# A hybrid decoder step: cache copies, low rank part and first loads moved in the RWKV stage

## The reference

```python
prev = concatenate([shift0[:, None, :], pa[:, :-1]], axis=1)
m = pa + (prev - pa) * mu
r, k, v, xw, xa, xg = split_last(m, A_SPLIT)
wlog = -softplus(-(w0 + tanh(xw) @ w2)) - 0.5
decay = exp(-exp(wlog))
a = sigmoid(a0 + xa @ a2)
g = sigmoid(xg) @ g2
...
S = S * w_t - s_kk * (kk_t * a_t) + v_t * k_t
y_t = S @ r_t
```

## Time and profile before

| what | us |
| --- | --- |
| three runs: median (lowest, highest) | 3149.25 (3148.3, 3158.02) |
| the profiled execution: its time, its span | 3146.62, 3144.8 |
| TensorE busy in the span | 2659.9 |
| VectorE, ScalarE, GpSimd busy | 1142.1, 666.5, 370.1 |

### The profile page before, as it was taken

One profiled execution on the slowest core, in us unless ns is written; L12 is line 12 of the kernel. 1 busy time (PEld: TensorE's weight loads), 2 busy tenths in 40 slices (PEclk: granted clock), 3 DMA queues, 4 the chain that ended last, 5 costly groups with the idle time before them and its releaser, 6 DMA issues. The chain is left out here.

```text
span 3144.8 us, 33977 instructions
## 1 busy us (share of the span) xinstructions
PE 2659.9 (85%) x13604; PEld 1693.4 (54%) x13604; DVE 1142.1 (36%) x2070; ACT 666.5 (21%) x1339; POOL 370.1 (12%) x352
## 2 busy tenths in 40 slices
PE   7999995084788888686647759999999999999998
PEld 3444441042567778354425425566666666888843
DVE  0007999565676664485704203200000000000033
ACT  1122221032334444474403200000000000000011
POOL 1000000102443441000016520000000000000000
PEclk9999997586799999798868879999999999999999
DMA  6111110322235343513779772311101102110010
GB/s 237 51 44 49 42 41 17 116 83 53 58 112 172 101 146 111 164 40 90 244 246 346 274 289 100 132 29 40 40 27 40 40 27 93 51 37 22 17 34 33
DMA packets 170291, 305.86 MB, mean 97 GB/s; under 512 B 48536, under 2 KB 121448, under 8 KB 167866
## 3 DMA queue, kind: packets, MB, share of 16 engines
q1 hardware_dynamic: 145154, 175.87, 17.9%
q0 software_dynamic: 23136, 93.01, 8.1%
q10 hardware_dynamic: 1864, 35.08, 3.2%
HBM read 262.76 MB, written 68.29 MB: 105 GB/s over the span
## 5 line engine op out<-in xcount | busy, mean ns | idle before, releaser
L929 PE MATMUL m_B<-m_big,m_wdB 128*128 128x363 f32 (+1 forms) x2112 | 646.0, 468 | 3.2 <-issue 3.2
L929 PEld LDWEIGHTS m_B<-m_big,m_wdB 128*128 128x128 f32 x2112 | 400.4, 190 | 247.9 <-issue 4.8
L384 PE MATMUL i_psM<-i_w,i_xnT 128*128 128x477 f32 x1024 | 418.3, 567 | 2.3 <-ACT i_xnT L232 2.3
L384 PEld LDWEIGHTS i_psM<-i_w,i_xnT 128*128 128x128 f32 x1024 | 192.8, 191 | 213.4 <-issue 206.5
L791 DVE TENSOR_TENSOR m_actT<-m_wdB,m_B 128x363 f32 (+3 forms) x66 | 35.1, 532 | 604.1 <-PE m_B L929 604.1
L683 ACT ACTIVATE m_wdB<-m_B 128x363 f32<-128x363 f32 (+1 forms) x66 | 31.2, 473 | 598.8 <-PE m_B L929 598.8
L971 PE MATMUL m_B<-m_wdA,m_actT 128*128 128x256 f32 x704 | 152.4, 379 | 0.8 <-DVE m_actT L791 0.8
L971 PE MATMUL m_B<-m_wdB,m_actT 128*128 128x256 f32 x704 | 152.6, 379 | 0.0
L971 PEld LDWEIGHTS m_B<-m_wdA,m_actT 128*128 128x128 f32 x704 | 133.7, 190 | 19.5 <-DVE m_actT L791 1.4
L971 PEld LDWEIGHTS m_B<-m_wdB,m_actT 128*128 128x128 f32 x704 | 133.5, 190 | 18.8 <-issue 0.8
L649 POOL TENSOR_TENSOR m_rstd<-m_ms,m_half 128x1 f32<-128x1 f32 x18 | 10.0, 553 | 1133.0 <-DVE m_ms L759 1133.0
(11 more groups left out here) (410 smaller groups left out, 3599.9 us busy)
## 6 DMA issues: line engine op xcount, KB each, us to landing
b_Kp<-b_k SPq DMA_DIRECT2D x32, 512.0 KB, 10.9
b_Vp<-b_v SPq DMA_DIRECT2D x32, 512.0 KB, 11.4
o_bk<-b_k ACTq DMA_DIRECT2D x8, 2040.0 KB
o_bv<-b_v ACTq DMA_DIRECT2D x8, 2040.0 KB
i_w<-w_in POOLq DMA_DIRECT2D x8, 1908.0 KB, 29.9
proj<-i_stage SPq DMA_DIRECT2D x64, 238.5 KB, 2.0
m_wdB<-w_gate SPq DMA_DIRECT2D x22, 512.0 KB, 4.0
m_wdB<-w_up SPq DMA_DIRECT2D x22, 512.0 KB, 5.2
```

The source lines that it names most:

```text
L384: mm = nc.tensor.matmul(psM[:, c % 2, 0:CHW], xnT[:, t % 2, k, :], w[:, k, c * CHW:(c + 1) * CHW], start=(k == 0), stop=(k == KO - 1))
L929: mm = nc.tensor.matmul(B[:, bank, 0:r1 - r0], wgu[:, i, u, k, :], hnT[:, k, r0:r1], start=(k == 0), stop=(k == KO - 1))
```

## The change

Six edits, all in the mix phase:

1. `load_first` moves ahead of the table's store in the indexer, and the loads of the eight old states follow it there.
2. The first difference (VectorE) and its multiply by mu (GpSimd) move from the start of `phase_rwkv` into the indexer.
3. In ScalarE's tile the copy of W stands between B and q, and for j of 1 and up the low rank activations follow behind q.
4. The cache copies are issued behind the sigmoid of w, ahead of the levels, in place of the end of the tile.
5. `warm`, an exponential of one column, follows the gate's copy at level 2, so that the exponential table is loaded there.
6. TensorE's pieces 0, 1 and 2 of the next tile's low rank part each move one place later, and VectorE's copies `turned` move behind the masks.

```diff
+        self.st_in = sb("st_in", [P, 4, H_A, 64])
...
+    def load_states(self, sp):
+        for n in range(N_SEQ):
+            sp.dma_start(self.st_in[64 * (n % 2):64 * (n % 2) + 64, n // 2, :, :],
+                         self.D["wkv"][n].rearrange("h v k -> v h k")).then_inc(self.S["st_in"], 16)
+
+    def first_difference(self, dve):
+        dve.wait_ge(self.S["cur_in"], 16)
+        dve.wait_ge(self.S["prev_in"], 16 * (N_SEQ + 1))
+        self.nc.vector.tensor_tensor(self.prev[0:64, :], self.prev[0:64, :], self.cur[0:64, :], ALU.subtract)\
+            .then_inc(self.S["d"], 1)
+
+    def first_shift(self, pool):
+        pool.wait_ge(self.S["mu_in"], 16)
+        pool.wait_ge(self.S["d"], 1)
+        self.nc.gpsimd.tensor_tensor(self.prev[0:64, :], self.prev[0:64, :], self.mu[0:64, :], ALU.mult)\
+            .then_inc(self.S["dmu"], 1)
...
                 load(1)
-                for n in range(N_SEQ):
-                    sp.dma_start(st_in[64 * (n % 2):64 * (n % 2) + 64, n // 2, :, :],
-                                 D["wkv"][n].rearrange("h v k -> v h k")).then_inc(S["st_in"], 16)
...
-                pool.wait_ge(S["mu_in"], 16)
-                shift(0)
+                count["dmu"] = 1
...
+                def warm():
+                    f(tiny[:, :], half[:, 0:1], ACT.Exp)
...
-                    if nxt:
-                        lora_of(j + 1)
-                    evac_bq(j)
+                    if j == 0:
+                        lora_of(1)
+                    evac_bq(j, 0)
                     if j >= 1:
                         evac_w(first(old))
+                    evac_bq(j, 1)
+                    if j >= 1:
+                        if nxt:
+                            lora_of(j + 1)
                         evac_u(first(old), old, 0)
                         evac_y(first(old), old, 0)
...
                     if nxt:
                         sig_w(j + 1)
+                    if j >= 1:
+                        move_caches(j - 1)
                     for lev in range(last + 1):
...
                         if lev == 2 and nxt:
                             gate(j + 1)
+                            warm()
...
-                    if j >= 1:
-                        move_caches(j - 1)
...
-                differ(0)
                 select(1)
                 mix(0)
...
                     evac_pr(j)
+                    if j == 0:
+                        turned(1)
                     if nxt:
-                        turned(j + 1)
                         keys(j + 1)
                     mask(j)
+                    if j and nxt:
+                        turned(j + 1)
...
                     elif where == "turned2":
                         if j >= 1:
                             solve(old, 0)
-                        if nxt:
-                            front(j + 1, 0)
+                        elif nxt:
+                            front(1, 0)
                     elif where == "matted":
                         if j == 0:
...
+                            front(1, 1)
                         else:
+                            if nxt:
+                                front(j + 1, 0)
                             close(old, 0)
-                        if nxt:
-                            front(j + 1, 1)
                     elif where == (0, 0):
...
                         if nxt:
-                            front(j + 1, 2)
+                            front(j + 1, 1 if j else 2)
                     elif where == (0, 1):
                         if j >= 2:
                             old_part(old, 1)
+                        if nxt and j:
+                            front(j + 1, 2)
...
                 sp.dma_start(cmask[:, :], D["cmask"]).then_inc(cmask_in, 16)
+                mix_.load_first(sp)
+                mix_.load_states(sp)
                 sp.wait_ge(summed, TCH)
                 sp.dma_start(D["table"], table[:, :]).then_inc(table_out, 16)
-                mix_.load_first(sp)
...
+                mix_.first_shift(pool)
...
+                mix_.first_difference(dve)
                 for q in range(NQ):
```

More of the change, by code:

```diff
@@ L1079, in __init__ @@
         self.score = self.room[0:64, :]
-        names = "cur_in prev_in mu_in vec_in small_in lw_in last_in round unsel unsel_out score_out table_out".split()
+        self.st_in = sb("st_in", [P, 4, H_A, 64])
+        names = "st_in d dmu cur_in prev_in mu_in vec_in small_in lw_in last_in round unsel unsel_out score_out table_out".split()
         self.S = {n: nc.alloc_semaphore("a_" + n) for n in names}
         self.nc, self.D = nc, D
+    def load_states(self, sp):
[12 more added lines that the diff above has]
+            .then_inc(self.S["dmu"], 1)
     def load_first(self, sp):
@@ L1146, in phase_rwkv @@
         masks = [at("mask_s"), at("mask")]
-        half = sb("half", [P, H_A])
+        half, tiny = sb("half", [P, H_A]), sb("tiny", [P, 1])
         lora = sb("lora", [P, P])
@@ L1169, in phase_rwkv @@
         mean, var, rstd = (sb(n, [P, H_A]) for n in ("mean", "var", "rstd"))
-        st_in = sb("st_in", [P, 4, H_A, 64])
+        st_in = mix_.st_in
         STs = sb("STs", [P, 4, N_SEQ, 64])
@@ L1178, in phase_rwkv @@
         S = {n: sem(n) for n in (
-            "st_in n_in v_in d dmu m lora loraT lT z sig cum exps kk sq ssk "
+            "n_in v_in m lora loraT lT z sig cum exps kk sq ssk "
             "rsk kkn k2 p r b q rk bonus pown own owned bq pr evacB evacP mat mats LT1 L xt0 low vb lnb Wdone W Udone U Sdone "
@@ L1440, in exp_end, with evac_bq @@
                         .then_inc(S["exps"], 1)
-                def evac_bq(j):
+                def evac_bq(j, x):
                     n = chunks(j)
[L1444 to L1448, removed]
+                    act.wait_ge(S["bq"], 2 * j + x + 1)
+                    src = B[:, 2 + x, 0:256 * n].rearrange("p (i c t) -> p i c t", i=4, c=n)
+                    f(BQ[0:64, :, 0:n, x, :], src[0:64], ACT.Copy).then_inc(S["evacB"], 1)
+                    f(BQ[64:P, :, 0:n, 1 - x, :], src[64:P], ACT.Copy).then_inc(S["evacB"], 1)
+                def warm():
+                    f(tiny[:, :], half[:, 0:1], ACT.Exp)
                 def evac_w(k):
```

## The result

| | before | changed |
|---|---|---|
| first runs, median (lowest to highest), us | 3152.96 (3148.3 to 3158.02), 4 runs | 3128.36 (3124.85 to 3129.63), 4 runs |
| profiled execution's own time, us | 3146.62 | 3129.59 |
| its span, us | 3144.8 | 3127.8 |
| RWKV stage in it, us | 543.0 | 521.4 |

The account below looks back on a forecast made before the run. No engine fills the RWKV stage, so its order decides. Terms −3.5 − 10.8 − 3.5 + 0.4 − 1.9 give −19 on 3146.6, 3128, plus 1.3 toward the median: 3129 us; own range 3120 to 3139, stated range 3114 to 3144.

Parts of the forecast that it names:

- Indexer, nothing: Indexer: early loads, states, difference and multiply fit where engines already wait or idle; cost nothing.
- Start, −3.5: RWKV stage's start: VectorE's first difference (1.92) and wait (1.58) go, so m of the sample rows comes 3.5 us earlier.
- taken as worth nothing: Stage start: moving the state loads alone gains nothing, since one DMA engine carries the shifted rows; bounds 0 and 3.4 us.
- Tile 1, 0; tile 2, +0.4; tile 3, −3.5: Whole tiles: tile 1's 1.1 and 1.4 cancel; tile 2 loses 0.4 us; tile 3 gains 3.5, its start giving 3.8.
- Tiles 4 to 7, −2.7 each, −10.8: Each tile: start gains 3.0 us, exponential table 1.4; VectorE's low rank copies cost 0.6, moved low rank products 1.1.
- The cache copies, hidden by 1 us: ScalarE between sigmoid of w and first X copy: that copy ends at 3.2, TensorE wants it at 4.2.
- Tail, −1.9: Behind the last tile: TensorE's 2.01 us wait while ScalarE issues copies ahead of W goes, but for W's copy waiting its turn.
- the states were the wait: Rival, stage start: state packets hold up the shifted rows; moving them frees TensorE's 23.79 us too, 3105; chance 0.06.
- The tile start gains nothing: Rival, tile starts: half-speed products or VectorE eat the 3.0 us; 3146 against the median; chance 0.17.
- The clock stays up: Rival, tile starts: shorter idle leaves the clock at 1.00, masks another us earlier in tiles 3 to 7; 3122; chance 0.15.
- The half clock reaches into the levels: Rival, slower: half speed eats the 3.0 us and costs 3.4 in the levels of tiles 3 to 8; 3166; chance 0.07.
- The table load: Rival, ScalarE behind the gate: the load holds it as long again, exceeding the gap by 0.7 in seven tiles; 3134; chance 0.04.

Follow-up runs that it names:

- states_back: Changed kernel with the eight old-state loads put back behind the loads of tile 1, all else kept; 3127.74 us, ratio 0.9926.
- no_warm: Changed kernel without the one-column exponential behind the gate's copy; 3136.8 us, ratio 0.9955.
- lowrank_back: Changed kernel with the low rank part back in its old place on ScalarE, TensorE and VectorE; 3121.69 us, ratio 0.9903.
- copies_end: Changed kernel with the four cache copies issued at the end of a tile again; 3130.26 us, ratio 0.9938.
- start_only: Kernel before with only the start part: early first loads and states, first difference and its multiply in the indexer; 3150.72 us, ratio 0.9996.
- three: Changed kernel plus tile 1's shifted rows loaded in two parts, VectorE's last two finishing operations behind level 0, low rank part in its old place; 3082.29 us.
- split_load: Changed kernel with the shifted rows of tile 1 loaded as 112 and 15 rows instead of 127 in one; 3105.63 us, ratio 0.9858.

## Why the prediction was right, point by point

The number, the direction and what bounds the stage, TensorE's waits, were right; the steps less evenly so.

- *Indexer, nothing.* Right: the stage in front of RWKV ends 0.4 us later in the profiled execution (728.8 for 728.4), no more than the difference between executions: the kernels with the same indexer end it between 728.1 and 730.2.
- *Start, −3.5.* Measured −4.9: 3.4 from the difference and the wait, and 1.5 from the states, within their bounds of 0 to 3.4 (states_back: 1.6).
- *Tile 0.* Here the sum had no term, and this is the step that failed: the state move was "taken as worth nothing", by bounds that only allowed a gain. It cost: tile 0 got 3.3 us longer at half clock, and with the states put back the stage is 3.0 shorter, in the profiles; the times of the two kernels are the same (3128.36 and 3127.74 us). The turned states, which had stood behind TensorE's long wait, now stand ahead of it.
- *Tile 1, 0; tile 2, +0.4; tile 3, −3.5.* Measured 0, +0.9, −5.1. In tile 3 the start gave 4.0 us for the 3.8 forecast; the excess is clock, the B products took 3.68 us before and 2.06 now.
- *Tiles 4 to 7, −2.7 each, −10.8.* Measured −3.2, −2.9, −2.6 and −1.4, together −10.1. In tile 4 the terms show singly: start −2.9 for −3.0; exponential table −1.3 for −1.4 (no_warm: 8.4 us over the stage); the moved product +1.1, confirmed by lowrank_back. VectorE's low rank copies cost the 0.6 forecast: from the end of the masks to the first X it needs 1014.56 − 1012.71 = 1.85 us before and 1006.33 − 1003.85 = 2.48 now. The first X still comes 2.7 us earlier in the tile, because the B products took 0.43 us less, a term that the sum did not have. Over tiles 4 to 7 that term is −0.4, +0.2, +0.5 and +0.5, and tile 7's start gave only 2.0. VectorE, before and then in the changed kernel:

```profile
1014.56 0.68 DVE L1677 TENSOR_TENSOR a_X<-a_B,a_smalls 128x512 f32<-128x512 f32 x1
```

```profile
1002.56 1.29 DVE L1691 TENSOR_TENSOR a_mats<-a_B,a_smalls 128x512 f32<-128x512 f32 x2 [0.38 <-PE a_B L1845]
...
1006.33 0.67 DVE L1699 TENSOR_TENSOR a_X<-a_B,a_smalls 128x512 f32<-128x512 f32 x1
```

- *The cache copies, hidden by 1 us.* Right: they end at 1013.65 in tile 4 and no wait of TensorE is put down to X there; copies_end shows the same from the other side.
- *Tail, −1.9.* The wait of 2.01 us is gone, but tile 8 and the tail give 5.7 in all. Nearly all the rest is clock: the B products of tile 8 took 3.79 us before and 3.28 now, the sixteen products of its level 0 3.65 and 2.27, the products behind the tail's U 2.00 and 1.25, and the old-state products after them 1.80 and 1.15. The level 0 products, before and now:

```profile
1218.88 3.65 PE L1821 MATMUL a_B<-a_X,a_LT 128*128 128x128 f32 x16 [0.59 <-DVE a_X L1677]
```

```profile
1202.32 2.27 PE L1845 MATMUL a_B<-a_X,a_LT 128*128 128x128 f32 x16 [0.58 <-DVE a_X L1699]
```

So the overshoot at the start, in tile 3 and in the tail and the missing loss in tile 0 nearly cancel: −21.6 for −19 in the stage. The forecast also stood on 3147.9 us for the kernel before, 2 to 5 us under its later medians, which hides the rest. That the time came out within 1 us of 3129 is luck to that extent. That the change gains some 20 us is not: 15.2 of the 21.6 lie in tiles 3 to 7, for which 14.3 were forecast.

Of the rivals, "the states were the wait" fell in the profile and in start_only. "The tile start gains nothing" fell: 2.9 us in tile 4. "The clock stays up" is half true of this change (the fall at tile 4's start lasts 3.4 us instead of 6.8) and, in tiles 3 to 7, wholly true of three, where the B products start 1.1 to 1.8 us behind the transposes of p. "The half clock reaches into the levels" happened in tile 0 alone, with 8.2 us more at half clock; no other tile got more than 3.4. The table load was no longer than its 1.28: the one-column exponential starts 0.02 us behind it, so the drain that the Trainium skill ("ScalarE: Activation LUTs", What ACT_TABLE_LOAD costs) adds is again in no row. The Trainium skill's rule that a 127-partition transfer gets a single DMA engine ("DMA: Bandwidth & Descriptors", Why a DMA increments its semaphore by 16 and not by 1, which is its section, not the one that the prediction names) agrees with split_load, where the 127 rows in two parts saved 19.9 us.

## What to carry to other kernels

Where an engine waits for one thing, ask what would be late next and by how much: the spare time behind it decides which of several moves are worth making, and a move that only fills the spare time (here the low rank part) should not put work into a place that has none. Read a slow load by its shape before moving other loads away from it; splitting one transfer took 19.4 us off the stage's start, four times the 4.9 that moving the loads and the first difference took off it. And when a wait is shortened or moved ahead of other work, look at the granted clock of the stretch behind it, in both kernels, before calling a product slower or faster.

## What the runs showed that was not expected

Work moved from behind a long wait into it need not gain, and here went with a loss: with the states turned at 777.72, behind an idle time of 23.83 us, the products of tile 0 took 30.95 us; with them turned at 753.04, ahead of 23.01 us idle, 37.01. That is one profile each, and its cause is open. And short waits pay twice: where TensorE waits 0.8 us at the start of tile 4 instead of 3.1, the B products take 2.06 us instead of 2.87. In the kernel three, whose clock stays up, tiles 4 to 7 come out alike to 0.01 us (44.31 or 44.32 each).
